# The memory's norm, keys and values between two experts of the second mixture, and another order at the start of the convolution

## The chip, the cores and the metric

The kernel runs on one core of a Trainium2 chip. The metric is the device time of one execution in microseconds (us). TensorE (PE), VectorE (DVE), ScalarE (ACT), GpSimd (POOL) and SyncE (SP, which here issues nearly all loads) run beside each other and wait for each other by semaphores; 16 DMA engines move data.

## The reference

Three blocks follow each other on x of 256 x 1024, all in float32. Block 0 is a differential attention with a mixture of experts, block 1 a short convolution with a mixture of experts, and the last block a parallel mixer (an mLSTM beside a causal attention), a cross attention to a memory, and a feed-forward. The parts that matter:

```python
def ec_moe(h, w_router, w_gate, w_up, w_down):          # 16 experts, 32 rows each
    aff = softmax(h @ w_router); g, idx = top_k(aff.T, cap); xs = h[idx]
    a = silu(xs @ w_gate) * (xs @ w_up)
    y = (a @ w_down) * g
    return zeros.at[idx].add(y)

def odd_mixer(h, w_in, conv_w, w_out):
    bg, cg, u = split(h @ w_in, 3)
    return (bg * shortconv(cg * u, conv_w)) @ w_out

# last block, one layer
x = x + parallel_mixer(rmsnorm_2(x, norm_mix_g), ...)
h = rmsnorm_2(x, norm_x_g)
mem_n = rmsnorm_2(mem, norm_mem_g)                       # mem: 256 x 1024, an input
q = rmsnorm_2((h @ wq_x) by heads, xq_norm_g)
kv = mem_n @ wkv_x                                       # 1024 x 1024, 4 heads of 128
k = rmsnorm_2(kv[:, 0], xk_norm_g); v = kv[:, 1]
x = x + softmax(q k^T / sqrt(128)) v @ wo_x
x = x + square(relu(rmsnorm_2(x, norm_ffn_g) @ w_ff1)) @ w_ff2
```

The memory's norm, its keys and its values depend on inputs alone, not on x.

## The kernel before, in words

**Weights.** A ring of 12 slots in SBUF holds units of weights of 1 MB. `weight_units` lists the units in the order of their use, and SP issues the loads in that order; before each, `room` waits until the unit that had the slot has been read. An expert of a mixture is exactly 12 units: 4 of w_gate, 4 of w_up, 4 of w_down. `moe0` and `moe1` stand in the list for all loads of a mixture. At its head the units of expert 1 go to tiles outside the ring ("extras", `extra`, 10 in the first mixture and 11 in the second), as soon as what stood there is no longer used (`left`); `turn_of` says behind which of expert 0's units which extras are issued. From expert 3 on SP runs in a loop, and load s of an expert waits for the semaphore `MOE_READ`, which PE raises once per unit, to say that unit s of the expert before has been read.

**A mixture.** `pe_moe`, and `moe` of DVE and of ACT, run experts 0 and 1 unrolled and the others in loops of 2 to 5 and 6 to 15 (`BREAK` = 6). Per expert PE gathers rows of x (L889), transposes them (L894), multiplies with gate and up (L904, 8 units of 16 instructions), transposes (L913, L918), multiplies with down (L927, 4 units) and adds the weighted result to four open banks (L940). In the first mixture some work on the modulation (`pe_ada_cols`, `pe_gate`, `pe_router_bias`) stands at the break.

**The convolution.** Its weights and rows are split in two float32r parts: ACT rounds a unit (`round_weights`, L2336), DVE takes the rest (`rest_of_weights`, L1662), PE makes three products. At its start ACT squares x (`squares_of_x`), rounds unit 0, rounds the rows h1 in eight chunks (L2484), rounds unit 1, and copies moe_gate out of its bank (`moe_gate_out`, L2292). DVE makes diag, the rest of unit 0, half of h, the rests of h1 in four pairs, and then the rest of unit 1. PE's first product conv_c.0 (L749) takes these as they come, in the bank in which moe_gate stood.

**The last block.** The memory is loaded behind in2.1 into a spare slot. ACT and DVE norm it (`squares`, L2238; `norm_rows`), PE transposes it (L553, `nm`) behind in2.1, and DVE and ACT scale it into memT. The keys and values are four units `kvx` of w_kv, 256 columns each: kvx.0 before PE waits for `qk_ready` (the normed and rotated queries and keys), kvx.1 before it waits for `hm_ready` (the normed mLSTM output), kvx.2 and kvx.3 in four parts (L1267) between the steps of the causal attention (`pe_attend` with `beside_attention`). ACT copies them out (`keys_values`), DVE sums the squares of kx in `beside_b`, the roots are taken together with those of oa, ACT scales kx, and PE transposes it (kxT) behind out2.1. Per tile of the attention: PE score (L1280, L1281), DVE mask and maximum (L2070, L2073), ACT exp (L2616), PE transpose (L711), ACT copy (L2625), PE product (L718). Beside it ACT rounds and DVE takes the rest of the output projection's weights (`round_late`, `rest_late`).

## Time and profile before

| | us |
|---|---|
| median of 3 runs | 1650.56 (1647.87 to 1651.27) |
| profiled execution | 1647.83 |
| its span, first to last instruction | 1646.0 |
| PE busy in it | 1320.1 (80%) |
| DVE busy | 574.1 (35%) |
| ACT busy | 369.2 (22%) |
| HBM read | 546.29 MB, mean 333 GB/s |

The page gives busy times of the engines, then their busy tenths in 40 slices of 41.15 us, with the TensorE clock that was granted and the DMA engines' share. The first mixture lies at about 264 to 707 us, the convolution at 707 to 821, the second mixture at 821 to 1269, the last block behind it. A timeline has one line for a run of like instructions: start, duration, engine, line of the kernel, output and inputs, count, and in brackets how long the engine had been idle and what it waited for.

### The profile page before, as it was taken

The page shows a single profiled execution, that of the slowest core. Times are in us where ns is not written, and L with a number is a line of the kernel's source. Part 1 is how long each engine was busy: PE and PEld are TensorE (multiplying, and loading weights), DVE is VectorE, ACT ScalarE, POOL GpSimd, SP SyncE. Part 2 cuts the span into 40 slices and gives each one's busy share as a digit, 9 for nine tenths or more (in the row PEclk, how much of TensorE's full clock was granted, in tenths as well). Part 3 has the DMA queues.
Part 4 walks back from the last instruction along what each step waited for, and adds up shares of the span by engine and source line. Part 5 has one row for each costly group of instructions (what it writes and reads, how often), then busy time and mean ns, then how long its engine had stood idle before and what let it go on. Part 6 is the DMA issues. An engine that isn't in the chain of part 4 may idle for free. (4 is left out here: it accounts for less than half of the span.)

```text
span 1646.0 us, 30136 instructions
## 1 busy us (share of the span) xinstructions
PE 1320.1 (80%) x12594; PEld 893.8 (54%) x12594; DVE 574.1 (35%) x1200; ACT 369.2 (22%) x648; POOL 28.0 (2%) x54
## 2 busy tenths in 40 slices
PE   5899997877667576679977566676676999899999
PEld 3798584433323232269844222322333878889997
DVE  3575664101101011047531101100101676875555
ACT  3423432000000000044410000000001435564443
POOL 3020100000000000000000000000000000000000
PEclk8999999977887878799999978868878999999999
DMA  9998799999999999996799999999999742455640
GB/s 329 367 311 303 254 404 394 420 422 422 420 423 421 422 422 422 422 363 194 263 420 414 422 421 421 422 422 422 422 422 405 238 136 70 129 179 185 198 155 26
DMA packets 146083, 548.45 MB, mean 333 GB/s; under 512 B 9758, under 2 KB 77760, under 8 KB 97112
## 3 DMA queue, kind: packets, MB, share of 16 engines
q1 hardware_dynamic: 143360, 542.97, 84.0%
q10 hardware_dynamic: 1080, 3.64, 0.6%
q0 software_dynamic: 1568, 0.77, 0.4%
q8 instruction: 56, 0.92, 0.2%
q14 instruction: 19, 0.16, 0.0%
HBM read 546.29 MB, written 1.05 MB: 333 GB/s over the span
## 5 line engine op out<-in xcount | busy, mean ns | idle before, releaser
L904 PE MATMUL bank<-ring,scratch 128*32 128x256 f32 x3840 | 300.5, 464 | 143.3 <-DMA ring<-in_moe_w_up 96.9
L904 PEld LDWEIGHTS bank<-ring,scratch 128*32 128x32 f32 x3840 | 134.1, 128 | 294.9 <-DMA ring<-in_moe_w_up 148.8
L927 PE MATMUL bank<-ring,scratch 128*32 128x256 f32 x1968 | 156.1, 465 | 55.2 <-DMA ring<-in_moe_w_down 41.3
L1614 DVE COPY scratch<-bank 128x256 f32<-128x256 f32 x32 | 13.6, 425 | 426.6 <-PE bank L913 426.6
L779 PE MATMUL bank<-scratch_split,ring_split 128*128 128x256 f32 x1248 | 145.5, 277 | 1.8 <-DVE ring_split L1662 1.8
L779 PEld LDWEIGHTS bank<-scratch_split,ring_split 128*128 128x128 f32 x1248 | 144.6, 188 | 3.5 <-DVE ring_split L1662 2.0
L927 PEld LDWEIGHTS bank<-ring,scratch 128*32 128x32 f32 x1968 | 65.2, 130 | 139.0 <-DMA ring<-in_moe_w_down 70.6
L1662 DVE TENSOR_TENSOR ring_split<-ring,ring_split 128x2048 fp32r<-128x2048 f32 x48 | 110.0, 2292 | 75.8 <-ACT ring_split L2336 75.7
L2319 ACT ACTIVATE scratch<-bank 128x256 f32<-128x256 f32 x32 | 12.3, 384 | 481.8 <-PE bank L904 481.8
L2336 ACT CAST ring_split<-ring 128x2048 fp32r<-128x2048 f32 x48 | 91.5, 1905 | 57.4 <-PE bank L1340 36.8
L1621 DVE TENSOR_TENSOR scratch<-bank,moe_gate 128x256 f32<-128x256 f32 x32 | 13.6, 425 | 239.9 <-PE bank L927 239.9
L1340 PE MATMUL bank<-ring_split,scratch_split 128*128 128x512 f32 x384 | 90.7, 392 | 0.5 <-DVE scratch_split L2210 0.5
L614 PE MATMUL bank<-ring_split 128*128 128x256 f32 x480 | 86.1, 283 | 3.6 <-DVE ring_split L1654 3.5
L1340 PEld LDWEIGHTS bank<-ring_split,scratch_split 128*128 128x128 f32 x384 | 70.9, 188 | 15.5 <-issue 1.1
L614 PEld LDWEIGHTS bank<-ring_split 128*128 128x128 f32 x480 | 73.0, 188 | 6.0 <-issue 6.0
L2315 ACT COPY scratch<-bank 128x256 f32<-128x256 f32 x32 | 11.9, 372 | 285.7 <-PE bank L889 285.7
L574 PE MATMUL bank<-ring,hT 128*128 128x256 f32 (+1 forms) x320 | 68.9, 375 | 0.6 <-ACT hT L2280 0.6
L574 PEld LDWEIGHTS bank<-ring,hT 128*128 128x128 f32 x320 | 59.6, 190 | 8.4 <-issue 1.2
L940 PE MATMUL bank<-scratch 32*128 32x256 f32 x512 | 43.0, 455 | 20.4 <-DVE scratch L1621 19.2
L671 PE MATMUL bank<-ring,cond 128*32 128x256 f32 x768 | 50.7, 403 | 7.5 <-DMA ring<-in_ada_w 5.9
L1595 DVE TENSOR_TENSOR scratch<-bank,gain 128x128 f32<-128x128 f32 x64 | 15.6, 286 | 100.6 <-PE bank L894 100.5
L940 PEld LDWEIGHTS bank<-scratch 32*128 32x128 f32 x512 | 28.6, 211 | 36.3 <-issue 36.0
(465 smaller groups left out, 1576.4 us busy)
## 6 DMA issues: line engine op xcount, KB each, us to landing
ring<-in_moe_w_down SPq DMA_DIRECT2D x123, 1024.0 KB, 26.4
ring<-in_moe_w_gate SPq DMA_DIRECT2D x120, 1024.0 KB, 24.8
ring<-in_moe_w_up SPq DMA_DIRECT2D x120, 1024.0 KB, 26.6
ring<-in_ada_w SPq DMA_DIRECT2D x48, 1024.0 KB, 9.5
ring<-in_w_ff SPq DMA_DIRECT2D x32, 1024.0 KB, 5.3
ring<-in_conv_w_in SPq DMA_DIRECT2D x12, 1024.0 KB, 12.0
ring<-in_attn_w_in SPq DMA_DIRECT2D x10, 1024.0 KB, 11.5
ring<-in_w_in SPq DMA_DIRECT2D x7, 1024.0 KB, 12.3
```

The source lines that it names most:

```text
L574: mm = nc.tensor.matmul(T[:, t * 256:t * 256 + width], lhs[:, k, t * P:(t + 1) * P], W[:, k, :], start=(k == ks[0]), stop=(k == ks[-1]))
L614: mm = nc.tensor.matmul(T[:, t * 256:t * 256 + 256], ht[:, k, t * P:(t + 1) * P], wt[:, k, :], start=(k + i == 0), stop=(k == KD - 1 and i ...
L671: mm = nc.tensor.matmul(T[32 * j:32 * j + 32, c0:c0 + 256], cond[:, k, :], W[:, a, j * 256:j * 256 + 256], start=(k == 0), stop=(k == 7))
L779: mm = nc.tensor.matmul(T[:, m * SEQ:(m + 1) * SEQ], wt[:, k, m * P:(m + 1) * P], ht[:, k, :], start=(k + i == 0), stop=(k == KD - 1 and i ...
L904: mm = nc.tensor.matmul(GU[32 * j:32 * j + 32, m * 256:(m + 1) * 256], xs[:, k % 2, 16 * k - k % 2 * 16:16 * k - k % 2 * 16 + 32], W[k % 2 ...
L927: mm = nc.tensor.matmul(Y[32 * g:32 * g + 32, 0:256], actT[:, b, 32 * j:32 * j + 32], W[b][:, g * 256:(g + 1) * 256], start=(j + b == 0), ...
L940: mm = nc.tensor.matmul(banks[4 + g][:, t * 256:(t + 1) * 256], comb[32 * g:32 * g + 32, t * P:(t + 1) * P], y_s[32 * g:32 * g + 32, :], s ...
L1340: mm = nc.tensor.matmul(acc[2 * t + c][:, :], ht[:, u % 2, a, t * P:(t + 1) * P], wt[:, a, c * 512:(c + 1) * 512], start=(u + a + i == 0), ...
L1595: ins = V.tensor_tensor(own, T[:, b * P:(b + 1) * P].rearrange("p (g c) -> p g c", g=4), bc(gain[:, l, 2, b::2].unsqueeze(2), [P, 4, CAP]) ...
L1614: V.tensor_copy(comb, banks[1][:, 256:512]).then_inc(comb_ready, 1)
L1662: give("w_split", V.tensor_tensor(lo[n % 2], ring[:, q, :], hi[n % 2], ALU.subtract))
L2336: sig("w_hi").give(A.copy(w_parts[p][0][n % 2], ring[:, q, :]))
```

## The change

- The memory is loaded into scratch behind expert 2's loads of the second mixture, and w_kv in four row blocks of 256 x 1024 (`mem_w`, in tiles that expert 1 has left) between the loads of experts 5 and 6. The `kvx` units are gone from the list, so the later units take other slots.
- `pe_memory`, and `memory` of DVE and ACT, run between experts 5 and 6 of the second mixture: norm, 16 transposes, 32 matmuls of 512 columns into banks 0 to 3, the norm of the keys, 8 transposes into kxT. The results stay behind the table of constants (kx, kxT, vx). In the last block all steps on the memory go, with their waits; `nxt` is moved on so that the banks stay as they were. The float32r rests hm_lo and h3_lo take a spare slot of the ring.
- At the start of the convolution ACT rounds unit 0 before the squares, and copies moe_gate and rounds unit 1 before the chunks; DVE takes the rest of unit 1 before the last two rests of h1.
- In the second mixture extra 10 is issued behind expert 0's first unit, extras 3 and 4 behind its seventh, instead of behind the eighth.

```diff
-    cols("kvx", w["wkv_x_2"][0], 0, [256] * 4)
...
-        kxT, qx = carve(S, 32, 4, SEQ), carve(S, 36, TT, 512)
+        qx = carve(S, 36, TT, 512)
...
-        mem_raw, mem_n, memT = carve(spare[0], 0, TT, D), carve(spare[1], 0, TT, D), carve(spare[2], 0, KD, SEQ)
-        kx, vx = carve(spare[3], 0, TT, 512), carve(spare[3], 4, TT, 512)
+        mem_raw, mem_n, memT = carve(S, 42, TT, D), carve(S, 34, TT, D), carve(S, 0, KD, SEQ)
+        mem_w = [z.rearrange("p (a n) -> p a n", a=2) for z in (mid, rows_tile, turned_tile, table_tile)]
...
         at_free = TABLE_COLS / 256.0
+        kx, kxT, vx = carve(TB, at_free, TT, 512), carve(TB, at_free + 4, 4, SEQ), carve(TB, at_free + 8, TT, 512)
+        low_rows = ring_split[:, (base[2] + 3) % SLOTS, :]
...
-        hm_hi, hm_lo = HTR[:, 0:4, :], carve(TBR, at_free + 8, 4, SEQ)
+        hm_hi, hm_lo = HTR[:, 0:4, :], carve(low_rows, 4, 4, SEQ)
...
-        h3_hi, h3_lo = HTR, carve(TBR, at_free + 4, KD, SEQ)
+        h3_hi, h3_lo = HTR, carve(low_rows, 0, KD, SEQ)
...
@@ -826,6 +827,39 @@
...
+
+        def pe_memory(pe):
+
+            sig("xn_ready").take(pe)
+            sig("xn2_ready").take(pe)
+            for b in range(4):
+                T = tile(pe, f"nm.{b}", bank=b)
+                for i in range(4):
+                    k = 2 * b + i // 2
+                    mm = nc.tensor.transpose(T[:, i * P:(i + 1) * P], mem_n[:, i % 2, k * P:(k + 1) * P], ident)
+                done(f"nm.{b}", mm)
+            for b in range(4):
+                copied(pe, f"nm.{b}")
+            acc = [[tile(pe, f"kv.{t}.{n}", bank=2 * t + n) for n in range(2)] for t in range(TT)]
+            for k in range(KD):
+                if k % 2 == 0:
+                    pe.wait_ge(loads[f"mem_w{k // 2}"], 16)
+                for t in range(TT):
+                    for n in range(2):
+                        mm = nc.tensor.matmul(acc[t][n][:, :], memT[:, k, t * P:(t + 1) * P],
+                                              mem_w[k // 2][:, k % 2, n * 512:(n + 1) * 512],
+                                              start=(k == 0), stop=(k == KD - 1))
+                        if k == KD - 1:
+                            done(f"kv.{t}.{n}", mm)
+            sig("kx_ready").take(pe)
+            for b in range(2):
+                T = tile(pe, f"kxT.{b}", bank=2 * b)
+                for i in range(4):
+                    k = 2 * b + i // 2
+                    mm = nc.tensor.transpose(T[:, i * P:(i + 1) * P], kx[:, i % 2, k * P:(k + 1) * P], ident)
+                done(f"kxT.{b}", mm)
+            for name in ("kv.0.1", "kv.1.1", "kxT.0", "kxT.1"):
+                copied(pe, name)
 
         def pe_gate_spread(pe, l, bank=None):
 
@@ -954,6 +988,8 @@
                 pe_router_bias(pe, 1, bank=2)
                 for name in ("gate1.2.0", "gate1.2.1", "rb1"):
                     copied(pe, name)
+            else:
+                pe_memory(pe)
             with pe.Fori(BREAK, NEXP) as e:
...
-            pe_turn_rows_after(pe, "nm", mem_n)
+            nxt[0] += 4
...
-            for b in range(4):
-                copied(pe, f"nm.{b}")
-            pe_natural(pe, ("kvx", 0), "kvx.0", memT, KD, 256)
-
+            nxt[0] += 1
...
-            pe_natural(pe, ("kvx", 1), "kvx.1", memT, KD, 256)
+            nxt[0] += 1
...
-                if 1 <= i <= 4:
-                    u, t = 2 + (i - 1) // 2, (i - 1) % 2
-                    W = slot(pe, ("kvx", u), KD, 256)
-                    T = banks[place[f"kvx.{u}"][0]] if t else tile(pe, f"kvx.{u}")
-                    for k in range(KD):
-                        mm = nc.tensor.matmul(T[:, t * 256:t * 256 + 256], memT[:, k, t * P:(t + 1) * P], W[:, k, :],
-                                              start=(k == 0), stop=(k == KD - 1))
-                    if t:
-                        done(f"kvx.{u}", mm)
-                        unit_done_with(("kvx", u), f"kvx.{u}")
+                if i in (1, 3):
...
+            def memory():
+
+                v.wait_ge(loads["mem"], 16)
+                norm_rows(mem_raw, mem_n, ss_ctx)
+                turned("nm", memT, plain("norm_mem_g_2"), (0, 2))
+                for t in range(TT):
+                    sig("kx_squares").take(v)
+                    sq = carve(S, 34 + 2 * t, 4, P)
+                    ins = V.tensor_reduce(ss24[:, 8 + 4 * t:12 + 4 * t], sq, AX, ALU.add)
+                step(ins)
+                give("mean_ready", V.tensor_scalar(ss24[:, 8:16], ss24[:, 8:16], 1.0 / P, EPS, ALU.mult, ALU.add))
+                sig("root_ready").take(v)
+                step(V.reciprocal(ss24[:, 8:16], ss24[:, 8:16]))
+                for t in range(TT):
+                    T = product(v, f"kv.{t}.0")[:, :].rearrange("p (h d) -> p h d", d=P)
+                    empty(v, f"kv.{t}.0", V.tensor_tensor(
+                        kx[:, t, :].rearrange("p (h d) -> p h d", d=P), T,
+                        bc(ss24[:, 8 + 4 * t:12 + 4 * t].unsqueeze(2), [P, 4, P]), ALU.mult))
+                give("kx_ready", V.tensor_copy(st[:, 247:248], ident[:, 0:1]))
+                turned("kxT", kxT, lambda k: (vcol("xk_norm_g_2"), None), (0,))
 
             def moe(l):
...
+                else:
+                    memory()
...
+                if b == 2:
+                    rest_of_weights(0, 1)
                 pair = slice(2 * b, 2 * b + 2)
                 copied(v, f"n1.{b}")
                 give("h_split", V.tensor_tensor(h1_lo[:, pair, :], hT[:, pair, :], h1_hi[:, pair, :], ALU.subtract))
-            rest_of_weights(0, 1)
...
-            v.wait_ge(loads["mem"], 16)
-            norm_rows(mem_raw, mem_n, ss_ctx)
...
-                elif i == 2:
-                    for n in range(2):
-                        copied(v, f"kvx.{n}")
-                    norm4_sums(kx, sq2, 0, ss24, 8)
-                elif i == 3:
-                    norm4_sums(kx, sq2, 1, ss24, 8)
...
-            def squares_of_x(parts, updated=None, turns=None):
-
-                load_table(ACT.Sqrt)
+            def squares_of_x(parts, updated=None, turns=None, table=True):
+
+                if table:
...
+            def memory():
+
+                load_table(ACT.Sqrt)
+                s.wait_ge(loads["mem"], 16)
+                squares(mem_raw, mem_n, ss_ctx)
+                turned("nm", memT, plain("norm_mem_g_2"), (1, 3))
+                for t in range(TT):
+                    T = product(s, f"kv.{t}.0")
+                    sig("kx_squares").give(A.activation(carve(S, 34 + 2 * t, 512), T[:, :], ACT.Square))
+                roots(ss24[:, 8:16], 8)
+                for t in range(TT):
+                    T = product(s, f"kv.{t}.1")
+                    empty(s, f"kv.{t}.1", A.copy(vx[:, t, :], T[:, :]))
+                turned("kxT", kxT, lambda k: (vcol("xk_norm_g_2"), None), (1,))
+                load_table(ACT.Silu)
+
...
-            squares_of_x(2, "moe_acc0")
+            load_table(ACT.Sqrt)
             s.wait_ge(MOE_READ, 12 * NEXP)
             round_weights(0, 0)
+            squares_of_x(2, "moe_acc0", table=False)
+            moe_gate_out(1)
+            round_weights(0, 1)
...
-            round_weights(0, 1)
-            moe_gate_out(1)
...
-            s.wait_ge(loads["mem"], 16)
-            s.wait_ge(MOE_READ, 12 * (2 * NEXP - 1) + 2)
-            squares(mem_raw, mem_n, ss_ctx)
...
-            sig("heads_scale").take(s)
-            for t in range(TT):
-                for h in range(4):
-                    own = kx[:, t, h * P:(h + 1) * P]
-                    ins = A.activation(own, own, ACT.Copy, scale=ss24[:, 8 + 4 * t + h:9 + 4 * t + h])
-            sig("kx_ready").give(ins)
-            turned("kxT", kxT, lambda k: (vcol("xk_norm_g_2"), None), (1,))
...
-                    turn_of = ({4: (2, 3, 4), 8: (5,), SLOTS: (6, 7, 8, 9)}, {TAIL: (10, 3, 4), SLOTS: (5, 6, 7, 8, 9)})[l]
+                    turn_of = ({4: (2, 3, 4), 8: (5,), SLOTS: (6, 7, 8, 9)}, {1: (10,), 7: (3, 4), SLOTS: (5, 6, 7, 8, 9)})[l]
...
-                    with sp.Fori(3, NEXP) as e:
-                        for s in range(SLOTS):
-
-                            sp.wait_ge(MOE_READ, e * 12 + (12 * (e0 - 1) + s + 1))
-                            load_expert(l, e, s)
+                    if l == 1:
+                        sp.dma_start(mem_raw, w["mem_2"][0].rearrange("(t p) d -> p t d", p=P)).then_inc(loads["mem"], 16)
+                    for first, end in ((3, BREAK), (BREAK, NEXP)):
+                        if l == 1 and first == BREAK:
+                            for u in range(4):
+                                sp.dma_start(mem_w[u], w["wkv_x_2"][0][256 * u:256 * u + 256, :].rearrange(
+                                    "(a p) n -> p a n", p=P)).then_inc(loads[f"mem_w{u}"], 16)
+                        with sp.Fori(first, end) as e:
+                            for s in range(SLOTS):
+
+                                sp.wait_ge(MOE_READ, e * 12 + (12 * (e0 - 1) + s + 1))
+                                load_expert(l, e, s)
...
-                    sp.dma_start(mem_raw, w["mem_2"][0].rearrange("(t p) d -> p t d", p=P)).then_inc(loads["mem"], 16)
```

## Rows read from the trace of the kernel before

**Rows 1.** The page, part 2: busy tenths and granted clock in 40 slices of the span

```profile
PE   5899997877667576679977566676676999899999
PEclk8999999977887878799999978868878999999999
DMA  9998799999999999996799999999999742455640
```

**Rows 2.** Windows: stretch, us, busy us (count) of PE, PEld, DVE, ACT, POOL, clock, DMA share, GB/s

```profile
720.00:725.00 5.00, 3.90 (x22) 3.90 (x23) 2.50 (x2) 1.05 (x2) 0.00 (x0) 0.66 1.11 357
745.00:810.00 65.00, 62.61 (x534) 61.54 (x534) 45.24 (x51) 28.73 (x34) 0.00 (x0) 1.00 0.57 189
900.00:1240.00 340.00, 226.68 (x2630) 100.32 (x2630) 32.88 (x136) 13.16 (x35) 0.00 (x0) 0.81 1.01 422
```

**Rows 3.** Timeline of PE, experts 5/6 and 2/3: start, us, instruction, [idle before, releaser]

```profile
961.28 6.34 PE L927 MATMUL bank<-ring,scratch 128*32 128x256 f32 x64 [0.46 <-ACT scratch L2321]
996.43 1.07 PE L927 MATMUL bank<-ring,scratch 128*32 128x256 f32 x16 [1.25 <-DMA ring<-in_moe_w_down]
870.45 8.80 PE L904 MATMUL bank<-ring,scratch 128*32 128x256 f32 x128 [1.19 <-DVE scratch L1601]
890.16 8.80 PE L904 MATMUL bank<-ring,scratch 128*32 128x256 f32 x128 [1.19 <-DVE scratch L1601]
```

**Rows 4.** Timeline of SP's issues, then DMA issues of four windows (us to landing)

```profile
808.92 0.44 SPq L2767 DMA_DIRECT2D scratch<-in_moe_w_up  x1
816.45 1.75 SPq L2767 DMA_DIRECT2D ring<-in_moe_w_down  x4
ring<-in_conv_w_in SPq DMA_DIRECT2D x1, 1024.0 KB, 25.1
ring<-in_moe_w_up SPq DMA_DIRECT2D x1, 1024.0 KB, 4.9
scratch<-in_moe_w_up SPq DMA_DIRECT2D x1, 1024.0 KB, 11.4
```

**Rows 5.** Timeline of PE, the break between experts 5 and 6 of the first MoE

```profile
406.77 0.75 PE L687 MATMUL bank<-table,scratch 128*128 128x128 f32 x4
415.71 9.32 PE L904 MATMUL bank<-ring,scratch 128*32 128x256 f32 x128 [1.19 <-DVE scratch L1601]
```

**Rows 6.** Timelines of PE and ACT, start of the convolution

```profile
721.10 7.07 PE L749 MATMUL bank<-scratch_split,ring_split 128*128 128x256 f32 x48 [5.40 <-ACT moe_gate L2292]
710.93 1.88 ACT L2336 CAST ring_split<-ring 128x2048 fp32r<-128x2048 f32 x1
713.12 3.76 ACT L2484 ACTIVATE scratch_split<-bank,ada_col,gain 128x256 fp32r<-128x256 f32 x8 [0.31 <-PE bank L1115]
```

**Rows 7.** Timeline of ACT, the memory's norm scaled in the last block

```profile
1279.90 1.15 ACT L2238 ACTIVATE ring<-ring,st 128x1024 f32<-128x1024 f32 x1 [0.30 <-DVE st L1407]
```

**Rows 8.** Timeline of PE, last block up to the first attention

```profile
1287.51 1.91 PE L553 MATMUL bank<-table,ring 128*128 128x128 f32 x16
1348.10 7.07 PE L574 MATMUL bank<-ring 128*128 128x256 f32 x32
1364.75 1.04 PE L553 MATMUL bank<-table,scratch 128*128 128x128 f32 x8
1367.61 3.72 PE L1267 MATMUL bank<-ring 128*128 128x256 f32 x16
1387.16 0.33 PE L711 MATMUL bank<-table 128*128 128x128 f32 x1
```

**Rows 9.** Timeline of DVE, the same stretch

```profile
1334.58 0.36 DVE L1992 COPY st<-bank 128x2 f32<-128x2 f32 x4 [4.73 <-PE bank L1227]
1354.05 0.15 DVE L2048 COPY st<-table 128x1 f32<-128x1 f32 x1
1360.92 1.23 DVE L2061 TENSOR_TENSOR scratch<-scratch 128x1024 f32<-128x1024 f32 x1
1387.34 0.42 DVE L2070 TENSOR_TENSOR table<-bank,table 128x256 f32<-128x256 f32 x1 [2.42 <-PE bank L1281]
```

32 lines of the change are left out of this document (11 added, 21 removed).

## The prediction

> **What bounds the kernel now.** I read the page first. Part 2 shows two long stretches in which the DMA engines are at nine tenths in every slice while TensorE (PE) is at five to seven: the two mixtures of experts. Between them, in the convolution, and behind them, in the last block, it is the reverse [rows 1]. The windows give sizes: from 900 to 1240 us DMA moves 422 GB/s at a share of 1.01 while PE is busy for 227 of 340 us; from 745 to 810 us PE is busy for 62.6 of 65 us and DMA for 0.57 of it [rows 2]. Then the timelines. In the second mixture PE stops at a unit of weights that has not landed [rows 3]. One unit is 1,048,576 bytes, 2.485 us at 422 GB/s, and an expert is twelve of them, 29.8 us; where its weights have landed, one expert costs PE 890.16 - 870.45 = 19.7 us. So the second mixture ends when its bytes have come, and what stands in it is free only as long as DMA stays busy meanwhile. In the last block PE works almost without a gap, and only its own timeline beside VectorE's (DVE's) can tell what removed PE work brings [rows 8, 9].
>
> The sum is made against the profiled execution, 1647.83 us with a span of 1646.0; the median of the three runs shown is 1650.56, 2.7 us more. I add the change to the median.
>
> **1. Start of the convolution.** PE waits 5.40 us for conv_c.0, until 721.10, although the rows that it multiplies are rounded from 713.12 on: its bank is emptied by ACT's copy of moe_gate (L2292), which stands behind all rounding [rows 6]. The change puts that copy ahead. It also puts the rounding of the first weights ahead of the squares. That unit was issued at 681.35 and lands after 25.1 us, at 706.5 [rows 4]; the rounding (1.88 us) ends at 708.4 and the squares, which began at 707.74, begin 0.7 later, and with them the roots and diag. Moe_gate's copy and the second rounding then end at 714.0, the eight chunks (0.47 each) at 717.8. DVE: weights' rest to 714.8, two turned pairs to 717.0, the first two rests of h1 from 717.85 to 719.3, then the moved rest of unit 1 (2.3) to 721.6, and the last two rests to 723.0. PE follows with its last four matmuls and is through at 723.5, where it was through at 728.0. **-4.5 us**, between -5.5 (no delay of the squares) and -3.5. From there PE is the bound until the router, with every weight landed early, so this passes through.
>
> The wait also left PE's clock at 0.66 of full for 720 to 725 us, and the 48 matmuls took 7.07 us [rows 2, 6] where the same 48 take 5.47 later in the stage; that part is in the 4.5.
>
> **2. Head of the second mixture.** The extras 10, 3 and 4 of expert 1 are now loaded while DMA is at 0.57. Before, the last of them, issued at 808.92, landed 11.4 us later, at 820.3, and the unit behind it at 822.8; a unit issued alone lands after 4.9 us, so the one issued at 816.45 could land at 821.35 [rows 4]: -1.45. The memory itself (1 MB) now stands in this saturated stretch: +2.5. **+1.0**, between -1.2 (it falls where DMA had run nearly dry, before expert 3) and +2.5.
>
> **3. The stop between experts 5 and 6.** This is the largest term. At the end of expert 5, twelve units of expert 6 are outstanding and four units of w_kv stand ahead of them: 16 x 2.485 = 39.8 us of cover behind the last landing of expert 5, about 966.6 (a cycle of 29.8 before the landing at 996.43 [rows 3]). No row shows a stop this long. The break of the first mixture shows a short one: between 406.77 and 415.71 PE does other work and then finds all eight units landed, 128 matmuls at one go [rows 5], with DMA at its full rate. So a stop is covered while units are outstanding. Here PE's chain is, from 961.28 + 6.34 = 967.62 [rows 3]:
> - DVE's y 0.5; then mean, root, reciprocal and scaling, whose row in the last block ends 1.85 us after the mean began (1279.20 to 1281.05 [rows 7]): 970.05. ACT's squares are done by then.
> - 16 transposes, next work 1.75 us after their start [rows 8], and the last bank emptied 1.0 later: 972.9.
> - 32 matmuls of 512 columns. The same columns were 4 units of 32 instructions, 6.9 us each from start to start (kvx.0 at 1348.10 [rows 8]): 27.6, and 0.4 for a clock that may be down at first: 1000.9.
> - squares of the last keys, sum, root, reciprocal, two scalings of 0.69, eight transposes, one more emptying: 4.95. ACT reloads its table, +0.3. Expert 6 needs 3.3 to its first matmul on weights and 0.95 to its first read; 0.1 for SP; then a unit issued into an idle queue lands after 4.9: 1015.4.
>
> SP's first load of expert 7 is queued behind that first read, and all later loads behind it. Before, expert 7's first unit landed at 998.9. **+16.5 us**; DMA idles about 6.5 of them. If DMA never idled the price would be 9.9 (four units); if the chain met half clock for longer, as in 870.45's row (8.80 for 128 matmuls, which are 7.1 at 834.61, at full clock), up to 20. I take the chain, since each of its links is a row.
>
> Behind the stop PE has twelve landed units and needs 19.7 us for them against 29.8 of DMA, so it catches up in expert 7 and nothing more is lost. SP's split loop and the register waits cost nothing that a row shows.
>
> **4. The last block.** PE loses 1.75 (transposes) + 13.8 (kvx.0, kvx.1) + 14.2 (four parts of 3.72, 3.56 from start to start, in the attention) + 0.9 (kxT) = 30.7 us of work. What is late next:
> - The transposes: PE works on without a wait until 1334. -1.75.
> - kvx.0 and kvx.1 stood over DVE's chain, which runs without a gap from the emptying of the mLSTM products (1334.58) through qk_ready (1354.2) to hm_ready (1360.92 + 1.23 = 1362.15) [rows 9]. It moves only by the 1.75. PE now waits 6.1 us for qk_ready and 5.0 for hm_ready; hmT starts at 1360.5 instead of 1364.75 [rows 8]. So of 13.8 us only 2.5 are saved. -4.25 so far.
> - The attention: from hmT (1364.75) to the transposes of tile 4 (1387.16) it took 22.4 us with the four parts [rows 8]. Without them the order score, mask and maximum, exp, transpose is bound by DVE and ACT: hmT 0.9, ACT's rounding of it 1.6, five tiles at 0.8 to 1.1 of DVE and 0.6 of ACT each, and beside them DVE's rest of hmT (2.0) and four roundings of 1.04 on ACT. Placed one by one tile 4 is turned 11.8 after hmT's start: 10.6 of the 14.2 saved, **-14.85** in all at full clock.
> - The clock. PE waited 5.4 us before 721.10 and then ran at 0.66 for that 5 us window [rows 2, 6]; here it waits 6.1 and 5.0 and goes on with short work. At half clock the scores and transposes of the first tiles put tile 4 some 2.9 later: -12.0.
> - From 1387.34 DVE has no gap until the output projection [rows 9], so the shift stands. Removing kxT and the scaling of kx from behind it gives 0.2, since x_ready is next.
> **-12.7 us**, between -15.0 (clock stays up) and -10; I take the value near the slow end because the waits are as long as the one whose price the row shows.
>
> The Trainium skill, "TensorE: Matmul & The Clock Gate", section "HAM oscillation - how this bites in real kernels", speaks against this change in the same place: waits between bursts put the array back at half rate and each burst then starts slow. By that rule the tail would give 12.0 rather than 14.85; the trace agrees at 721.10.
>
> **Sum:** -4.5 + 1.0 + 16.5 - 12.7 = +0.3 us. Profiled 1648.1, median **1650.9**.
>
> **The rivals.**
> A, the stop is covered. PE work that stands in a DMA-bound stage costs only its bytes: 16.5 becomes 9.9, and the whole comes to -6.3 us, 1644.3. For it: the first mixture's break, where DMA never slowed; and the steps around the 27.6 us of matmuls may overlap more than I let them. The chain would have to resume within 39.8 - 4.9 + 2.5 us. Against it: 27.6 + 4.95 + 5.3 alone is 37.9 before expert 6 has begun. Beside it: the Trainium skill, "Perfetto Trace Analysis", section "Optimization Strategy", says that a kernel with several regimes may gain from interleaving them; by that rule this is the result, 1644.3. Chance 0.27.
> B, half clock, on the other side. PE's light work with waits (the norm's steps, the head of kv, the attention without its filling, 1361 to 1385 us) runs at 1.2 GHz. The kv stage then costs 20 instead of 16.5, and the attention gives 4 less, since its scores, transposes and products (2.8 us of PE for two tiles at full clock, 5.2 at half) become longer than the DVE and ACT steps beside them: 1650.9 + 3.5 + 4 = 1658.4. It decides against the change once the clock is at half for some 6 us more than I count in those places together (3 us of cost). For it: 0.81 in the mixture, 0.66 after one wait. Against: PE at 1.00 in the later slices with waits of up to 2.2 us. Chance 0.2.
> C, the attention does not shorten because ACT's roundings and DVE are its bound at some 3 us a tile: 4.5 us less saved, 1655.4. Against it: tiles 5 and 6, without filling, come 1.9 us apart. Chance 0.08.
> D, the last block gives its whole 30.7, as it would if PE alone bound it: 18 more, 1632.9. DVE's gapless chain speaks against it. 0.03.
> The forecast 0.42.
>
> **How the numbers follow.** A measurement of this kernel can tell about 0.2%, 3.3 us, from no change. The forecast lies within it, with 3 us either side from the bounds of terms 1, 2 and 4. Faster: A and D, 0.30. Slower: B and C, 0.28. Same: 0.42. The range takes in A with its own spread below and B above: 1641.5 to 1660.0; D and the far end of B are left out.
>
> **What would show it.** Conv_c.1 starts near 723.5. In a stop of some 45 us between experts 5 and 6 DMA is idle for 4 to 9 us near its end; a gapless 422 GB/s there means A. Expert 6 then runs 128 matmuls at one go. The second mixture ends 13 us later than before, at about 1281.7 (L940's last end was 1268.8). PE waits about 6 and 5 us ahead of qk_ready and hm_ready; clock 1.00 right behind means -15, 0.5 there for long means B. From the mixture's end to the end of the span it is 12.7 us shorter. The prediction is wrong if the kv matmuls take other than 27 to 30 us, or if the loads queue otherwise than in order.

## The result and the profile after

The changed kernel takes 1661.57 us in the median of four runs (1658.77 to 1663.49), the kernel before 1650.91 beside it. The ratio is 1.0064, 95% interval 1.0048 to 1.0081: 10.6 us slower, where the prediction said 0.3, and above the range's end of 1660.0. The profiled execution is the slowest of the four (1663.49, span 1661.7), so stage times below are compared between profiled spans (1646.0 and 1661.7, +15.7), and what they add up to is checked against ratios of many runs further down.

Part 1 and, of part 2, the granted clock, the DMA share and the GB/s, which answer to [rows 1]:

```profile
PE 1334.6 (80%) x12530; PEld 895.7 (54%) x12530; DVE 574.5 (35%) x1203; ACT 370.1 (22%) x645; POOL 27.9 (2%) x54
...
PEclk8999998988867787899998788788788995999999
DMA  9998799999999999996699997999999840455640
GB/s 324 367 312 306 253 407 395 420 422 422 422 421 421 422 422 422 413 360 208 266 419 420 422 418 310 422 422 421 422 421 419 290 127 1 127 170 187 195 159 26
```

Two slices differ from before. The 25th has DMA at 7 and 310 GB/s in the middle of a mixture that had 9 and 414 to 422 there. The 34th has PEclk 5: TensorE (PE) near its lower clock for a whole slice of 41.5 us, where before no slice was under 6, and none behind the second mixture under 8.

**The stop.** PE's timeline from the end of expert 5 (start, duration, engine, line, operands; in brackets the idle time and what ended it), and below it SP's, which issues the loads:

```profile
968.87 1.07 PE L961 MATMUL bank<-ring,scratch 128*32 128x256 f32 x16 [0.30 <-DMA ring<-in_moe_w_down]
970.58 1.15 PE L974 MATMUL bank<-scratch 32*128 32x256 f32 x16 [0.64 <-DVE scratch L1665]
972.29 1.94 PE L839 MATMUL bank<-table,scratch 128*128 128x128 f32 x16 [0.57 <-DVE scratch L1442]
975.48 7.11 PE L849 MATMUL bank<-scratch 128*128 128x512 f32 x16 [1.25 <-ACT scratch L2317]
...
996.15 7.03 PE L849 MATMUL bank<-table,scratch 128*128 128x512 f32 x16
1006.12 1.97 PE L859 MATMUL bank<-table 128*128 128x128 f32 x8 [2.94 <-DVE st L1573]
1009.37 1.94 PE L923 MATMUL bank<-x,scratch 128*32 128x256 f32 x16 [1.28 <-ACT table L2317]
...
1013.68 9.84 PE L938 MATMUL bank<-ring,scratch 128*32 128x256 f32 x128 [1.19 <-DVE scratch L1645]
```

```profile
956.12 4.62 SPq L2843 DMA_DIRECT2D table<-in_wkv_x  x1
...
975.06 10.20 SPq L2803 DMA_DIRECT2D ring<-in_moe_w_down  x4
1015.87 4.74 SPq L2803 DMA_DIRECT2D ring<-in_moe_w_gate  x4
```

The products take what the sum gave them, 27.6 us, from 975.48 (972.9 in the sum; expert 5 ended 2.3 us later than before). Behind them the 8 transposes take 1.97 us and the 16 gathers of the next expert 1.94, as long as twice as many did at the upper clock. SP issues nothing between 985 and 1015.87, because its first load of expert 7 waits for expert 6's first read. The same stretch in windows (busy time of PE, PEld, DVE, ACT, POOL, then granted clock, DMA share, GB/s):

```profile
1005.00:1010.00 5.00, 2.60 (x16) 1.98 (x20) 2.07 (x6) 2.01 (x4) 0.00 (x0) 0.56 0.45 184
1010.00:1015.00 5.00, 3.33 (x33) 1.18 (x26) 1.52 (x8) 0.90 (x3) 0.00 (x0) 0.50 0.00 0
1015.00:1020.00 5.00, 5.00 (x60) 2.49 (x56) 0.00 (x0) 0.00 (x0) 0.00 (x0) 0.57 0.61 200
1020.00:1025.00 5.00, 4.05 (x71) 2.10 (x64) 0.76 (x2) 0.38 (x1) 0.00 (x0) 1.00 0.96 360
```

Of these 20 us, the missing shares of the four rows are 5 x (0.55 + 1.00 + 0.39 + 0.04) = 9.9 us without transfers. The second mixture ends 23.9 us later than before. Its last combining products, before and after:

```profile
1266.69 2.09 PE L940 MATMUL bank<-scratch 32*128 32x256 f32 x16 [0.64 <-DVE scratch L1621]
```

```profile
1290.54 1.15 PE L974 MATMUL bank<-scratch 32*128 32x256 f32 x16 [0.65 <-DVE scratch L1665]
```

**The last block.** These rows answer to [rows 8]:

```profile
1353.98 13.98 PE L575 MATMUL bank<-ring,hT 128*128 128x256 f32 x64
1373.95 3.68 PE L1275 MATMUL bank<-table,scratch 128*128 128x128 f32 x16 [5.99 <-DVE st L2092]
...
1382.20 1.97 PE L554 MATMUL bank<-table,scratch 128*128 128x128 f32 x8 [3.40 <-DVE scratch L2105]
...
1398.88 0.47 PE L712 MATMUL bank<-table 128*128 128x128 f32 x1
...
1404.34 3.78 PE L641 MATMUL bank<-ring_split,hT_split 128*128 128x256 f32 x16
...
1410.98 2.13 PE L641 MATMUL bank<-ring_split,hT_split 128*128 128x256 f32 x16
```

The same three things in the kernel before: the 16 transposes, the first late unit and the second (a late unit is one of the output projection, out2m.0, out2m.1 and so on):

```profile
1355.00 1.91 PE L1242 MATMUL bank<-table,scratch 128*128 128x128 f32 x16
...
1390.79 2.11 PE L640 MATMUL bank<-ring_split,hT_split 128*128 128x256 f32 x16
...
1396.13 2.13 PE L640 MATMUL bank<-ring_split,hT_split 128*128 128x256 f32 x16
```

The waits for qk_ready and hm_ready are there, 5.99 and 3.40 us (6.1 and 5.0 forecast). But the 16 transposes behind the first take 3.68 us instead of 1.91, the 8 behind the second 1.97 instead of 1.04, and the first half of the late unit (L641, 16 matmuls) 3.78 instead of 2.11. The window from 1374 to 1408 us says it in one number, a granted clock of 0.55, and PE busy for 30.1 of 34 us:

```profile
1374.00:1408.00 34.00, 30.11 (x106) 22.04 (x107) 24.56 (x56) 18.60 (x39) 0.00 (x0) 0.55 0.00 1
```

From the start of hmT, the 8 transposes of the mLSTM output, to out2m.1 the self-attention took 31.4 us before with four parts of kvx in it, and takes 28.8 now without them. The block gives back 8.2 us in these profiles (from +23.85 at the mixture's end to +15.6 at the feed-forward), of which 2.1 stood in the profile of before as half clock ahead of the block's first unit (there the last 16 combining products and the 16 transposes behind them took 2.09 and 3.67 us; here 1.15 and 2.45).

**The start of the convolution.** These answer to [rows 6]:

```profile
712.93 6.66 PE L1151 MATMUL bank<-scratch,x 128*128 128x128 f32 x32 [2.96 <-DVE scratch L1830]
...
726.57 8.64 PE L780 MATMUL bank<-scratch_split,ring_split 128*128 128x256 f32 x72
...
779.35 12.79 PE L780 MATMUL bank<-scratch_split,ring_split 128*128 128x256 f32 x96 [1.74 <-DVE ring_split L1708]
792.45 7.74 PE L795 MATMUL bank<-ring_split,scratch_split 128*128 128x256 f32 x63 [0.30 <-DVE ring_split L1708]
```

Conv_c.1 begins at 726.57, 1.4 us earlier than before and not 4.5. The 32 matmuls of n1, which turn the normed rows, take 6.66 us, where they took 3.84 before. At 779 two units take 12.79 us (11.34 before), and the first unit of the convolution's output begins at 792.45, 1.5 us later than before. On this profile alone the first term would be a loss.

### The profile page after: what moved, and what is told of

It reads as the page before. It is cut to its first block and busy times, and to the rows that moved or that the text cites. A ratio compares the mean times of both kernels' runs of the same rounds, so it can differ in the third digit from the quotient of the medians.

```text
span 1661.7 us, 30008 instructions
## 1 busy us (share of the span) xinstructions
PE 1334.6 (80%) x12530; PEld 895.7 (54%) x12530; DVE 574.5 (35%) x1203; ACT 370.1 (22%) x645; POOL 27.9 (2%) x54
## 5 line engine op out<-in xcount | busy, mean ns | idle before, releaser
L938 PE MATMUL bank<-ring,scratch 128*32 128x256 f32 x3840 | 294.4, 459 | 132.6 <-DMA ring<-in_moe_w_up 89.3
L961 PE MATMUL bank<-ring,scratch 128*32 128x256 f32 x1968 | 156.3, 464 | 54.9 <-DMA ring<-in_moe_w_down 40.5
L1639 DVE TENSOR_TENSOR scratch<-bank,gain 128x128 f32<-128x128 f32 x64 | 15.6, 286 | 102.4 <-PE bank L928 102.4
## 6 DMA issues: line engine op xcount, KB each, us to landing
ring<-in_moe_w_gate SPq DMA_DIRECT2D x120, 1024.0 KB, 24.1
```

The costliest lines, as they stand in the source:

```text
L938: mm = nc.tensor.matmul(GU[32 * j:32 * j + 32, m * 256:(m + 1) * 256], xs[:, k % 2, 16 * k - k % 2 * 16:16 * k - k % 2 * 16 + 32], W[k % 2 ...
L961: mm = nc.tensor.matmul(Y[32 * g:32 * g + 32, 0:256], actT[:, b, 32 * j:32 * j + 32], W[b][:, g * 256:(g + 1) * 256], start=(j + b == 0), ...
L1639: ins = V.tensor_tensor(own, T[:, b * P:(b + 1) * P].rearrange("p (g c) -> p g c", g=4), bc(gain[:, l, 2, b::2].unsqueeze(2), [P, 4, CAP]) ...
```

## The experiments

Fifteen kernels, each compared by its ratio to the kernel before, run beside it. Their medians of before lie between 1649.95 and 1651.75. Unless said otherwise, stage times are from PE's timeline.

### The parts one at a time

**The order alone** (kernel before with these edits, and VectorE's like those of the change):

```diff
-            squares_of_x(2, "moe_acc0")
+            load_table(ACT.Sqrt)
             s.wait_ge(MOE_READ, 12 * NEXP)
             round_weights(0, 0)
+            squares_of_x(2, "moe_acc0", table=False)
+            moe_gate_out(1)
+            round_weights(0, 1)
...
-            round_weights(0, 1)
-            moe_gate_out(1)
```

> The kernel before with the new order around the convolution alone: ScalarE rounds unit 0 ahead of the squares of x, the expert gate is copied out and unit 1 rounded ahead of the 16 chunks, VectorE's rest of unit 1 stands between its second and third h_split. The prediction's term says -4.5 us (-5.5 to -3.5) against the kernel before, with conv_c.1 starting near 723.5 us in place of 728.0. The trace of the changed kernel says otherwise: there the same instructions started at 726.6 (-1.4), after transposes at half the clock, and by the first unit of the convolution's output the lead was a lag of 1.5 us. Theory: the order leaves TensorE a wait that drops its clock, and the gain is at most 1.4 us here too (between -1.4 and +1.5). Rival: the half clock and the lag belong to that one execution, and this kernel shows -3 us or more.

Measured: ratio 0.9977 (0.9965 to 0.999), -3.8 us. Its profile, though, has n1 at 5.46 us, conv_c.1 at 724.98 (-3.0), 13.11 us for the two units behind the wait at 778, and the output's first unit at 790.96, exactly as before. So one profile of this stage does not tell its worth: the median says -3.8, within the prediction's -5.5 to -3.5. The loss that I read out of the changed kernel's profile was that execution's.

**The memory alone** (the changed kernel with those edits undone).

> The changed kernel with the convolution's old order; the memory's stop between experts 5 and 6, its freed last block and the new order of the extra tiles stay. By the prediction's terms it is 4.8 us slower than the kernel before (+1.0 +16.5 -12.7). By the trace of the changed kernel, with the convolution's lag of 1.5 us taken off, it is 12 to 14 us slower in the profiled execution and 8 to 12 us in the median. If the two parts are independent, this run and the one with the order alone add up to the changed kernel's +10.7 us.

Measured: 1.0088 (1.0069 to 1.0107), +14.5 us. With -3.8 it makes +10.7, and the changed kernel has +10.6: the two parts add up, as far as intervals of 2 to 3 us either side can show it. The prediction had +4.8 here; the miss is in this part.

**No memory at all**, which prices the stop with its bytes:

```diff
-            else:
-                pe_memory(pe)
...
-                else:
-                    memory()
+                else:
+                    V.memset(kxT, 0.0)
+                    V.memset(vx, 1.0)
...
-                    if l == 1:
-                        sp.dma_start(mem_raw, ...
-                            for u in range(4):
-                                sp.dma_start(mem_w[u], ...
```

> The changed kernel without any of the memory's work: no load of the memory or of its weights, no norm, no keys and values (keys are filled with 0, values with 1, so the last attention reads constants). What is left of the change is the convolution's order, the order of the extra tiles and the emptied last block. By the prediction's terms 1650.9 - 16.5 - 2.5 = 1631.9 us. By the trace of the changed kernel the stop and its bytes cost 22.7 us (5.2 MB at 420 GB/s is 12.5, and 10.2 us in which no transfer ran), which gives 1661.6 - 22.7 = 1638.9 us, 12 us under the kernel before; the last block gives back 8 us instead of 12.7. If the half clock in the last block were an accident of one execution, it would stand at 1634 or lower.

Measured: 0.9942 (0.9923 to 0.9961), -9.6 us. Against the changed kernel that is 0.0122, or 20.1 us for stop and bytes together; the prediction had 16.5 + 2.5 = 19.0. Its ten runs are spread from 1632 to 1646 us, so these differences are known to about 4 us. The last block of this kernel has the same half clock, with no stop anywhere in it:

```profile
1351.62 3.61 PE L1273 MATMUL bank<-table,scratch 128*128 128x128 f32 x16 [6.00 <-DVE st L2091]
...
1359.72 1.97 PE L554 MATMUL bank<-table,scratch 128*128 128x128 f32 x8 [3.40 <-DVE scratch L2104]
...
1388.45 1.74 PE L641 MATMUL bank<-ring_split,hT_split 128*128 128x256 f32 x13
```

28.7 us from hmT to out2m.1, as in the changed kernel (28.8). So the clock falls without any stop: it goes with the emptied block, though not always to the same depth (see the next run).

### The stop

**Two of eight product steps:**

```diff
-            for k in range(KD):
-                if k % 2 == 0:
-                    pe.wait_ge(loads[f"mem_w{k // 2}"], 16)
+            for k in (0, KD - 1):
+                pe.wait_ge(loads[f"mem_w{k // 2}"], 16)
```

> The changed kernel with 2 of the 8 steps of the products that make keys and values (the other 6 are left out); all loads, norms and transposes stay. The products shrink from 28.1 us to about 7.0, and the stop by 21.1. Theory: the stop costs its bytes (12.5 us) and the 10.2 us in which the queue stood; a stop of some 26 us is shorter than what the ring holds, so only the 10.2 goes, to 1651.4 us, and no gap is left in the DMA row. Rival: the experts behind are bound by TensorE and its chain, so the whole 21.1 goes, to 1640.5.

Measured: 0.9998 (0.9983 to 1.0012), 10.9 us less than the changed kernel for products that are 21 us shorter. DMA has 405 to 433 GB/s in each of 40 slices from 940 to 1040 us; the windows where the gap was:

```profile
980.00:985.00 5.00, 1.09 (x8) 0.86 (x8) 3.29 (x9) 2.31 (x6) 0.00 (x0) 0.91 1.01 415
985.00:990.00 5.00, 3.20 (x26) 1.26 (x30) 1.52 (x8) 1.66 (x3) 0.00 (x0) 0.50 1.01 421
```

In the second PE is at half clock and no transfer time is lost by it. Only the gap goes, and the bytes stay. In its last block, emptied like the others, the 8 transposes of hmT took 1.09 us, the clock was 0.66 behind them, and the attention took 24.7 us (1368.02 to 1392.73): of the five profiles with an emptied and unfilled block, the four others have 28.7 to 28.8. This profile also has the convolution that the first term described: n1 at 3.84 us, conv_c.1 at 723.03, the output's first unit at 787.29 (-3.7).

```profile
712.11 3.84 PE L1150 MATMUL bank<-scratch,x 128*128 128x128 f32 x32 [2.95 <-DVE scratch L1829]
...
723.03 7.23 PE L780 MATMUL bank<-scratch_split,ring_split 128*128 128x256 f32 x60
```

**Two stops**, with nothing left out: the keys between experts 5 and 6, the values' products between experts 9 and 10.

```diff
-            with pe.Fori(BREAK, NEXP) as e:
+            if l == 1:
+                with pe.Fori(BREAK, 10) as e:
+                    expert(e)
+                pe_memory_products(pe, 1)
+                for t in range(TT):
+                    copied(pe, f"kv.{t}.1")
+            with pe.Fori((BREAK, 10)[l], NEXP) as e:
                 expert(e)
```

> The changed kernel with its stop in two: norm, transposes, keys and the keys' transposes between experts 5 and 6, the values' products (14 us) between experts 9 and 10. Nothing is left out. Theory: only the time in which no transfer runs (10.2 us) and the bytes (12.5 us) cost; each stop is now shorter than what the ring holds, so the gap goes and the bytes stay: 10 to 11 us faster than the changed kernel, as with the shortened products (1650.3), 1650.5 to 1651.5. Rival: a second stop costs its own length because the ring is not full again by expert 9; then the gain is under 3 us.

Measured: 1.0006 (0.9989 to 1.0023), 9.6 us less than the changed kernel. PE does the same products. Where the gap was, the first stop's end runs at 423 GB/s; from 940 to 1120 us, with both stops in it, no slice is under 407:

```profile
995.00:1000.00 5.00, 3.45 (x30) 1.72 (x34) 1.52 (x8) 0.32 (x1) 0.00 (x0) 0.50 1.02 423
```

So the stop's 20.1 us are some 10 for a gap, by two independent edits, and 1.0006 - 0.9942 = 0.0064, 10.6 us, for moving 5.2 MB of memory and weights where DMA is the bound (12.5 us at 420 GB/s). The stage itself says the same more sharply. From the convolution's output to the end of the second mixture the profiles have:

| | us | profiles |
|---|---|---|
| memory not in the mixture | 475.4 to 476.4 | 7 |
| one stop | 498.1 to 498.3 | 4 |
| two stops | 487.9 to 489.5 | 5 |
| one stop with two of eight steps | 487.0 | 1 |

So the one stop and its bytes cost 22.5 us there: 10 for the gap and 12.5 for the bytes. The second stop, of 14 us, adds between 1 and 3 us to what the shortened one took.

### The last block

Here PE's waits are filled with matmuls that nobody reads, in the bank that kvx had: spin(n) is n products of 512 columns.

```diff
+            spin(pe, 12)
             sig("qk_ready").take(pe)
...
+            spin(pe, 7)
             sig("hm_ready").take(pe)
...
+                if 1 <= i <= 4:
+                    spin(pe, 4, i % 2)
```

> The changed kernel, with products of 512 columns that nobody reads put where the memory's products stood in the last block: 12 (5.3 us) ahead of the wait for qk_ready, 7 (3.1 us) ahead of the wait for hm_ready, 4 (1.8 us) in each of steps 1 to 4 of the self-attention. They add only work that lies inside TensorE's waits. Theory: the last block gave back less than was forecast because TensorE ran at half its clock from the qk transposes to the first late unit (28.8 us from the transposes of hm to out2m.1, against 31.4 before, with 14.9 us of products gone). At full clock the transposes return to 1.9 us and the attention takes 21 to 24 us: 7 to 10 us faster than the changed kernel, 1652 to 1655. Rival: the attention is held by VectorE and ScalarE, and the clock only fills their waits; then the gain is at most 3 us (1658.5 or more).

Measured: 1.012 (1.0086 to 1.0154), 9 us slower than the changed kernel. Neither theory had this. The rows show a size that I had wrong:

```profile
1364.00 10.46 PE L837 MATMUL bank<-x,table 128*128 128x512 f32 x24
1374.30 1.91 PE L1284 MATMUL bank<-table,scratch 128*128 128x128 f32 x16
...
1383.15 1.04 PE L554 MATMUL bank<-table,scratch 128*128 128x128 f32 x8
...
1414.44 1.74 PE L641 MATMUL bank<-ring_split,hT_split 128*128 128x256 f32 x13
```

Twelve products are 24 instructions and 10.46 us: 0.87 us each, not 0.44. The filling overran the first wait, and the transposes behind it began 24.1 us after the in2 units ahead of it, not 20.0; and it put 14.8 us into an attention that had lost 14.9, which then took 31.3 us, as before. But the clock was 1.00 throughout and both groups of transposes were at full speed (1.91, 1.04). So filling holds the clock; it was too much of it.

**Light filling on the kernel with two stops**: 6, 3 and 1 for 12, 7 and 4.

> The kernel with two stops, with fewer unread products than in the run that had 12, 7 and 4: one of 512 columns takes 0.87 us there, not 0.44, so that run put 14.8 us into an attention that had lost 14.9, and overran the first wait by 4.5 us. Here 6 (5.2 us) stand ahead of qk_ready, 3 (2.6 us) ahead of hm_ready, and 1 (0.9 us) in each of steps 1 to 4 of the self-attention. Theory: the half clock is what kept the emptied attention at 28.8 us; with the clock at its upper level through the two waits and a little work in the steps, it takes 31.3 - 11.4 = 20 to 24 us, and the kernel is 5 to 10 us faster than the one with two stops (1651.2), at 1641 to 1646. Rival: the clock falls in the attention all the same because its steps are too thin, and the gain is that of the transposes alone, 1 to 3 us (1648 to 1650).

Measured: 0.9965 (0.995 to 0.998), 6.8 us less than with two stops alone, and 5.8 less than before.

```profile
1363.15 1.97 PE L1293 MATMUL bank<-table,scratch 128*128 128x128 f32 x16 [0.85 <-DVE st L2113]
1371.10 1.10 PE L554 MATMUL bank<-table,scratch 128*128 128x128 f32 x8 [2.31 <-DVE scratch L2126]
1374.02 1.12 PE L850 MATMUL bank<-x,table 128*128 128x512 f32 x2
...
1392.74 2.08 PE L641 MATMUL bank<-ring_split,hT_split 128*128 128x256 f32 x16
```

21.6 us from hmT to out2m.1 against 28.7, with more work in it. This is the decisive run: PE does 11.3 us more than in the kernel with two stops, nobody reads it, and the kernel is faster. VectorE and ScalarE do the same as there, so they did not hold the attention at 28.7.

**Twice the filling in the steps**, 6, 3 and 2:

> As the run with one unread product in each of steps 1 to 4, with two (1.7 us in each, 7.0 in all). Theory: if one holds the clock, this is up to 3.5 us slower than that run; if one doesn't hold it and two do, the attention takes 31.3 - 7.9 = 23.4 us and this is the faster of the two, 5 us under the kernel with two stops. Rival: neither holds it and this run is at 1650 or above.

Measured: 0.9979 (0.9961 to 0.9997), 2.3 us over one each. Its attention takes 24.5 us at full clock (1371.58 to 1396.07), 2.9 longer than with one, near what four more products cost (3.5). One in each step is enough in that profile, and in that of the run further down with everything together (21.6 us again).

**The light filling on the changed kernel itself:**

> The changed kernel itself, one stop as it is, with the unread products that gave 6.8 us on the kernel with two stops: 6 ahead of qk_ready, 3 ahead of hm_ready, 1 in each of steps 1 to 4 of the self-attention. The run with 12, 7 and 4 overran its waits. Theory: the price of the half clock in the emptied last block is independent of the stop, so this kernel is 6 to 8 us faster than the changed one, at 1653.5 to 1655.5 us, and only 3 to 5 us slower than the kernel before; its attention from the transposes of hm to out2m.1 takes 21.6 us as there, not 28.8. Rival: behind the long stop the last block falls to half clock elsewhere, and the gain is under 3 us (1658.5 or more).

Measured: 1.0044 (1.003 to 1.0059), 3.3 us under the changed kernel's 1.0064: between theory (6 to 8) and rival (under 3). The intervals overlap, so the size is loose. Its profile shows why it is less: the clock fell in the first steps in spite of the filling, and again in the second attention.

```profile
1371.00:1403.00 32.00, 28.41 (x139) 18.60 (x139) 24.16 (x56) 19.65 (x42) 0.00 (x0) 0.89 0.00 1
1440.00:1450.00 10.00, 7.21 (x36) 5.45 (x34) 5.69 (x18) 5.98 (x16) 0.00 (x0) 0.83 0.34 105
```

Its attention took 24.4 us, between 21.6 and 28.8. In three profiles with this filling the clock held twice, in five without any it never did. The filling makes the drop rarer and does not exclude it.

### What the convolution's spread is

Ten unread products of 256 columns in place of five ahead of n1, on the order alone:

```diff
-                    for _ in range(5):
+                    for _ in range(10):
                         nc.tensor.matmul(T[:, 0:256], ident, x[:, 0, 0:256], start=True, stop=True)
                     sig("diag_ready").take(pe)
```

> The kernel before with the new order around the convolution alone, and 10 unread products of 256 columns in place of 5 ahead of the wait for the scaled diagonals. Of the five profiles with the new order, two had the 32 transposes of n1 at 3.84 us and two at 5.5 and 6.7, after a wait of 3.0 us; the old order, with a wait of 2.3 us, had 3.84 both times. Theory: longer cover keeps the clock, the transposes take 3.84 us each time, and the median is 0.5 to 1.5 us under that of the order alone (1645.5 to 1646.5). Rival: the other half-clock stretch at 778 us and the two rates of the split products make up the spread, and this kernel is the same as the order alone within 0.3 us.

Measured: 0.9968 (0.9951 to 0.9985), -5.3 us. PE's wait falls from 3.0 to 0.8 us and n1 takes 3.84. Over all profiles: with the new order and five products, n1 took 3.84 us in five executions and 5.46 to 6.66 in four; with ten, 3.84 in all six; with the old order, 3.84 in both. (Two of the expectations miscount the profiles they had by one.)

The same with the changed kernel's order of the extra tiles, and with two unread products of 512 columns ahead of unit 10 instead:

```diff
-                    turn_of = ({4: (2, 3, 4), 8: (5,), SLOTS: (6, 7, 8, 9)}, {TAIL: (10, 3, 4), SLOTS: (5, 6, 7, 8, 9)})[l]
+                    turn_of = ({4: (2, 3, 4), 8: (5,), SLOTS: (6, 7, 8, 9)}, {1: (10,), 7: (3, 4), SLOTS: (5, 6, 7, 8, 9)})[l]
```

> The order around the convolution with 10 unread products ahead of n1 (1644.35 us) and with the changed kernel's order of the extra tiles: tile 10 with unit 1, tiles 3 and 4 with unit 7. By the prediction's term the head of the second mixture is 1.45 us shorter with it: 1642.9. By the trace of the run without the memory it brings nothing: there the lag of 0.94 us at the start of the convolution's output was 0.90 us at the end of the mixture; then 1644.4. A loss would say that the earlier transfers hold up those of the convolution.

```diff
+                if n == 10:
+                    b = nxt[0] % 8
+                    pe.wait_ge(free[b], turns[b])
+                    for _ in range(2):
+                        nc.tensor.matmul(banks[b][:, :], ident, x[:, 0, 0:512], start=True, stop=True)
```

> The order around the convolution with 10 unread products ahead of n1, and 2 of 512 columns (1.7 us) ahead of the convolution's unit 10, where TensorE waits 1.8 to 2.0 us for VectorE. Of the ten profiles so far five had the two units behind that wait at 12.8 to 13.1 us (part of them at half clock) and five at 11.3 to 11.5. Theory: with the wait filled they take 11.4 us each time, and the median falls by 0.5 to 1.4 us to 1643 to 1643.9. Rival: the clock falls there for what came long before, and nothing changes (1644.4).

Measured: 0.995 (0.9934 to 0.9967) and 0.9948 (0.9927 to 0.9968). With the wait at 776 us filled the two units behind it took 11.34 to 11.36 us in all three profiles that have the filling; without it, 11.3 to 11.6 in nine and 12.8 to 13.1 in five. The tiles: from the output's first unit to the mixture's end the profile moves by -4.0 and -4.0, so nothing of the forecast 1.45 is seen in it. Taken over the seven profiles without the memory in the mixture, the stretch between the two takes 475.4 to 475.8 us in three profiles with the new order of tiles and 475.4 to 476.4 in four with the old.

All together, on both forms:

> Two stops, the light unread products in the last block (1645.35 us together, 0.35 % under the kernel before), and besides 10 unread products ahead of n1 and 2 ahead of the convolution's unit 10. Theory: the two half-clock stretches around the convolution go as they did with the old last block (there from 0.9977 to 0.9948 of the kernel before, with both), so this is 0.992 to 0.994, or 1638 to 1642 us. Rival: they were chance, and this is at 0.9965 again.

> The kernel before with the new orders alone (around the convolution and of the extra tiles), 10 unread products ahead of n1 and 2 ahead of unit 10; the memory stays in the last block. Each addition to the order alone came out at 0.9968 (10 ahead of n1), 0.9950 (with the tiles), 0.9948 (with unit 10). Theory: these three are one value within their intervals, the tiles and unit 10 bring under 1 us each, and this is at 0.995 (0.9935 to 0.9965). Rival: each brings 1.5 to 3 us of its own and this is at 0.993 or lower.

Measured: 0.9971 (0.9955 to 0.9986) and 0.997 (0.9955 to 0.9985), 1644.06 and 1644.82 us. Neither is under the runs with fewer additions. All six kernels between 0.9948 and 0.9971 have overlapping intervals, so what tiles and unit 10 add cannot be told.

Two stops with ten unread products ahead of n1 and the heavy filling of the last block:

> The changed kernel with all three: two stops, the unread products in the last block, 10 in place of 5 unread products ahead of n1. By the theory the gains add: 1661.6 less 10.5 for the gap, less 7 to 10 for the clock in the last block, less up to 1 at n1, or 1640 to 1644, which would beat the kernel before and the new order alone (1646.9). By the rivals it stays at 1650 or above.

Measured: 1.0048 (1.0031 to 1.0064). This kernel still had 12, 7 and 4 in the last block. Against two stops alone it is 6.9 us slower, as the same filling was 9 slower on one stop. The rival holds, for the filling's size and not for its own reason.

## Why the prediction was wrong

The sum's terms, each against the runs (a ratio of 0.001 is 1.65 us):

| Term | Forecast | Measured | From |
|---|---|---|---|
| 1 convolution's order | -4.5 | -3.8 | order alone |
| 3 stop, and the memory's bytes of term 2 | +16.5 +2.5 | +20.1 | changed kernel less no memory |
| 4 last block, and the tiles of term 2 | -12.7 -1.5 | -5.8 | no memory (-9.6) less term 1 |
| sum | +0.3 | +10.5 | changed kernel itself +10.6 |

The two lower rows hang on the run without the memory and are known to about 4 us each. Two readings of the profiles divide the miss better. The order of the tiles brought nothing, so its 1.45 us, which the table puts with the last block, were missed in the mixture. And the stage from the convolution's output to the mixture's end grew by 22.5 us, where terms 2 and 3 said +1.0 + 16.5 = 17.5. With 3.8 for the order that leaves some -8 for the last block. So of the 10 us missed about 5 lie in the mixture (1.5 for the tiles, 3.4 for a gap of 10 us where 6.6 was in the sum) and about 5 in the last block.

The sum had a slip of its own. The links of term 4 add up to -12.0 - 0.2 = -12.2, and -12.7 went in without a reason for the other half microsecond.

**Right, by its steps.** Bytes bound the mixture and PE the rest. The stop's chain held link by link up to the end of the products: norm to its end 2.35 us after expert 5 (2.4 forecast), emptying 3.2 later (2.9), products 27.6 (27.6). DVE's chain in the last block set qk_ready and hm_ready, so kvx.0 and kvx.1 gave 2.2 us from 1334 to hmT (19.70 to 17.45 later than before; 2.5 forecast). Rivals A (the stop covered) and D (all of PE's work saved) did not come.

**The step that failed: the clock's price in term 4.** I wrote that at half clock the scores and transposes "of the first tiles" put tile 4 some 2.9 later. Tile 4 is turned at 1398.88, 16.7 us after hmT, where I had 11.8 at full clock and 14.7 at half. Nor does it end there: the clock stays down to 1408, through the first 16 matmuls of the late unit, and once down PE, not DVE and ACT, is the bound of nearly every step (busy for 28.0 of the 29 us from 1382 to 1411). From hmT to out2m.1 the forecast at full clock was 31.4 - 10.6 = 20.8 us; the light filling showed 21.6 with 3.5 of filling in it. So the full-clock working was about right, and the half clock cost 7 us in this stretch instead of 2.9 (28.8 us against the 23.7 that the sum had for the half clock). From the transposes of qx to those of ox, in the second attention, where no kvx stood in either kernel, it took 17.1 us before and 18.5 after; part of this 1.4 is chance, since three of the six kernels with the old last block have 18.0 there, but all five with the emptied and unfilled one have 18.4 to 18.6. Rival B had this mechanism, at 4 us more than the forecast, and 3.5 in the stop. It gave 1658.4, the nearest of all to 1661.6, and should have been worked out to the end instead of for two tiles. The lower clock in the last block is shown as the cause on the kernel with two stops; on the changed kernel itself the filling gave only 3.3 us, by intervals that overlap.

The Trainium skill, "TensorE: Matmul & The Clock Gate", section "HAM oscillation - how this bites in real kernels", warned of bursts between waits, each starting slow. The trace agrees for both waits (3.68 for 1.91 us, 1.97 for 1.04), and goes further than I took it: PE, slow, was then 89% busy and still at 0.55.

**The second term that failed, the stop,** was mis-sized by the tail of its chain. From the end of the products (1003.2) to SP's next load (1015.87) it is 12.7 us, where the steps named make 9.6. The difference is half clock once more: transposes and gathers at nearly twice their time, and the 16 matmuls on weights ahead of the first read (2.2 us, where 0.95 was in the sum), so that DMA stood 10 us instead of 6.5. The shortened and the divided stop show that this gap is what the length costs.

**The order** was right in size, by twelve runs and not by its own profile. Where it adds a wait ahead of n1 (3.0 us, 2.3 before) it adds a chance of half clock, which the sum left out: in four of nine profiles, 1.6 to 2.8 us each.

What stays open: how much the clock is worth on the changed kernel itself (3.3 us there, 6.8 on two stops), and whether the order of the tiles brings anything. The ratios allow between nothing and 3 us, and the stage that it should shorten shows nothing.

## What to carry to other kernels

Work taken out of a matmul engine's waits is not saved at its own duration, and may be lost twice: it had also held the clock. If what stays is short work behind waits, cost the whole stretch at the lower clock until a long dense piece, and ask whether PE then becomes the bound; it can pay to put unread products back, sized from a row of the same shape: here a light filling gave 6.8 us and a heavy one lost 9. Work put into a transfer-bound loop costs its bytes plus only that part of its length which the outstanding loads do not cover: two stops that fit under the cover were 10 us cheaper than one that did not. And ask how well a number repeats before resting on it. The start of the convolution differed between profiles by as much as the edit was worth: the changed kernel's showed 1.5 us lost, where twelve runs of the order alone showed 3.8 gained. The mixture's length repeated to 0.3 us in four profiles, and told more than a difference of two ratios.

## What the runs showed of the hardware

**Two rates at one granted clock.** In the dense split products the granted clock is 1.00 in all seventeen profiles (from 730 to 774 us and from 1500 to 1600), yet the 48 matmuls of a feed-forward unit take one of two times for the whole stage; here the run with the memory alone, then the kernel before:

```profile
1508.38 5.82 PE L780 MATMUL bank<-scratch_split,ring_split 128*128 128x256 f32 x48
```

```profile
1504.75 5.63 PE L779 MATMUL bank<-scratch_split,ring_split 128*128 128x256 f32 x48
```

The stage, from its first unit of ff2 to its last, is 159.4 us in ten of the seventeen profiles and 162.3 in seven. The convolution has a like pair, 5.44 and 5.65 us a unit from start to start, and a profile can have either there and either in the feed-forward. That is 3 us of spread in the total that no edit here explains; the cause is open, and with one profile for each kernel it is not shown whether it goes with the execution or with the kernel.

**A wait of the same length drops the clock in some profiles and not in others.** Behind the 1.7 to 2.0 us wait at 776 us it fell in five profiles of fourteen, ahead of n1, behind 2.9 to 3.0 us, in four of seven. Filled with unread products, it fell in none.
